# Dealing the first block of an output projection between the products of the delta rule's last tiles (1 core)

## The reference

```python
u = rms_norm(h, norm_mix)
proj = u @ w_in
pool_out = pool_mixer(proj[..., :512], ...)          # 1024 tokens x 512
gdn_out = gated_delta_net(q, k, v, z, a, b, ...)     # 1024 tokens x 512, 4 heads of 128
mix = concatenate([pool_out, gdn_out], axis=-1)      # 1024 x 1024
h = h + mix @ w_out                                  # the output projection
```

## Time and profile before

| what | value |
|---|---|
| median of 3 runs | 2611.97 us (2608.75 to 2614.02) |
| the profiled execution | 2618.43 us, its span 2616.7 us |
| PE busy | 2405.8 us, 92% of the span, 13848 products |
| DVE busy | 1825.9 us, 70% |
| ACT busy | 1076.6 us, 41% |
| GpSimd (POOL) busy | 720.0 us, 28% |
| mean granted clock of TensorE | 0.968 of 2.4 GHz |

### The profile page before, as it was taken

One profiled execution on the slowest core, in us unless ns is written; L12 is line 12 of the kernel. 1 busy time (PEld: TensorE's weight loads), 2 busy tenths in 40 slices (PEclk: granted clock), 3 DMA queues, 4 the chain that ended last, 5 costly groups with the idle time before them and its releaser, 6 DMA issues.

```text
span 2616.7 us, 35014 instructions
## 1 busy us (share of the span) xinstructions
PE 2405.8 (92%) x13848; PEld 1916.5 (73%) x13848; DVE 1825.9 (70%) x2431; ACT 1076.6 (41%) x1616; POOL 720.0 (28%) x737
## 2 busy tenths in 40 slices
PE   3988968869999999999999999898799999999998
PEld 3966823557778787888886668677687878888887
DVE  5358988884588798877865783465327688777775
ACT  5135378743343334443343441233224334444433
POOL 1432277505555111111032223334162320000000
PEclk8999979989999999999999999899799999999999
DMA  6200154224223634555422110000231344555442
GB/s 232 73 17 17 41 156 116 88 65 137 73 65 113 220 127 168 177 177 187 139 89 75 38 40 25 2 2 26 93 92 57 117 173 154 193 177 177 169 145 81
DMA packets 173849, 282.19 MB, mean 108 GB/s; under 512 B 13407, under 2 KB 86900, under 8 KB 173686
## 3 DMA queue, kind: packets, MB, share of 16 engines
q1 hardware_dynamic: 159184, 255.38, 30.4%
q10 hardware_dynamic: 14502, 24.58, 2.6%
HBM read 252.52 MB, written 27.33 MB: 107 GB/s over the span
## 4 chain that ended last, share of the span: by engine, by line
PE 38%; DVE 7%; issue 2%; ACT 2%; POOL 1%; ACTq 0%; DVEq 0%; POOLq 0%
PE ps L2884 10%; PE ps L2873 9%; PE ps L2572 2%; PE ps L2587 2%; PE ps L2574 2%; PE ps L2573 2%; PE ps L2589 2%; PE ps L2588 2%; PE ps L3052 2%; DVE yt L2400 2%; DVE yt L2389 1%; PE ps L3116 1%; PE ps L3107 1%; PE ps L3110 1%; PE ps L3026 0%
## 5 line engine op out<-in xcount | busy, mean ns | idle before, releaser
L1447 ACT ACTIVATE w_hi<-raw 128x1024 fp32r<-128x1024 f32 x198 | 209.0, 1057 | 365.7 <-DVE raw L2120 160.5
L2103 DVE TENSOR_TENSOR w_lo<-raw,w_hi 128x1024 fp32r<-128x1024 f32 x198 | 258.9, 1308 | 126.4 <-ACT w_hi L1447 126.1
L2884 PE MATMUL ps<-w_hi,us_hi 128*128 128x512 f32 x784 | 308.8, 394 | 17.4 <-DVE u_f L2129 10.0
L2884 PE MATMUL ps<-w_lo,us_hi 128*128 128x512 f32 x784 | 307.8, 393 | 0.0
L2884 PE MATMUL ps<-w_hi,us_lo 128*128 128x512 f32 x784 | 307.5, 392 | 0.0
L2572 PE MATMUL ps<-h_hi,w_hi 128*128 128x512 f32 x704 | 286.5, 407 | 8.8 <-issue 4.3
L2573 PE MATMUL ps<-h_lo,w_hi 128*128 128x512 f32 x704 | 276.6, 393 | 0.0
L2574 PE MATMUL ps<-h_hi,w_lo 128*128 128x512 f32 x704 | 276.4, 393 | 0.0
L2153 DVE TENSOR_TENSOR x<-x,ps 128x512 f32<-128x512 f32 x392 | 247.8, 680 | 0.0
L2587 PE MATMUL ps<-w_hi,h_hi 128*128 128x512 f32 (+2 forms) x512 | 184.2, 360 | 18.8 <-DVE h_lo L2513 7.3
L1012 POOL TENSOR_TENSOR raw<-raw,gate 128x1024 f32<-128x1024 f32 x32 | 93.5, 2945 | 377.3 <-DMA raw<-in_w_down_dram 377.3
(11 more groups left out here) (472 smaller groups left out, 5273.0 us busy)
## 6 DMA issues: line engine op xcount, KB each, us to landing
h_all<-h_t SPq DMA_DIRECT2D x96, 512.0 KB, 5.6
h_extra<-h_t SPq DMA_DIRECT2D x96, 512.0 KB, 6.8
raw<-in_w_up_dram SPq DMA_DIRECT2D x64, 512.0 KB, 3.9
raw<-in_w_down_dram SPq DMA_DIRECT2D x64, 512.0 KB, 5.9
raw<-in_w_ada_dram SPq DMA_DIRECT2D x48, 512.0 KB, 4.4
raw<-in_w_in_dram SPq DMA_DIRECT2D x32, 512.0 KB, 3.8
raw<-in_w_out_dram SPq DMA_DIRECT2D x32, 512.0 KB, 3.8
h_t<-ht_hi ACTq DMA_DIRECT2D x32, 256.0 KB, 2.3
```

The source lines that it names most:

```text
L1447: s.activation(w_hi[:, slot, :], raw[:, r, :], ACT.Copy).then_inc(sem("w_hi_done"), 1)
L2103: v.tensor_tensor(w_lo[:, slot, :], raw[:, r, :], w_hi[:, slot, :].bitcast(F32), ALU.subtract).then_inc(sem("split_done"), 1)
L2884: last = mm(ps[:, b, :], l[:, c, tok], r, start=(fresh and c == 0 and n == 0), stop=(c == 1 and n == 2), skip_group_check=True)
```

## The change

The first of the four blocks (tokens 0 to 511, columns 0 to 511) leaves `out_proj`. Its 32 parts (a weight piece kk, a token tile i and a row k, three products each) are dealt out in TensorE's loop over `GSTEPS`, behind the steps that `OUT_AFTER` names, tiles 0 and 1 into the banks of tile 5, tiles 2 and 3 into those of tile 6. The second block follows in banks 2, 3, 6 and 7 (`OUT_BANK`), behind tile 7's last step. For this:
- the eight pieces of `mix` for tokens 0 to 511 are copied by ACT behind eight `level_z` steps of tiles 5 to 7 (`MIX_HI_AT`) into `out_hi`, which lies over the values and the second half of the keys, and subtracted by DVE behind the `level_tu` steps of the same tiles and levels (`MIX_LO_AT`), in place;
- the first four weight splits go into GpSimd's loop, behind its product in (level_z, 7, 1) to (level_z, 7, 4), the first with the two waits that stood behind the loop;
- x comes back through SP: four loads ahead of the projection's fifth weight, after tile 7 has used its queries; four ahead of its 13th, after the first half's eight output tiles are complete (`wo_full`);
- the eight pieces for tokens 512 to 1023 stay where all 16 were.

```diff
@@ -226,2 +226,4 @@
         pm = at("pm", [P, GH, S], F32, AD)
+        out_hi = [at("out_hi_p", [P, GH, S], F32R, AU), at("out_hi_z", [P, GH, S], F32R, AX_ + 16 * K1)]
+        out_lo = [at("out_lo_p", [P, GH, S], F32R, AD), at("out_lo_z", [P, GH, S], F32R, AU + 16 * K1)]
         yt = at("yt", [P, 2, S], F32, AD + 16 * K1)
@@ -504,2 +506,12 @@
+        OUT_BANK = (4, 5, 0, 1, 2, 3, 6, 7)
+        OUT_PARTS = [(i, kk, k) for pair in ((0, 1), (2, 3)) for kk in range(4) for i in pair for k in range(2)]
+        OUT_AFTER = {("level_tu", 6, 5): 4, ("finish_c", 5, 0): 1, ("level_tu", 7, 3): 1, ("tail_b", 6, 0): 2,
+                     ("level_z", 7, 4): 1, ("chunk_b", 6, 0): 1, ("chunk_b", 6, 1): 1, ("level_z", 7, 5): 1, ("level_tu", 7, 5): 4,
+                     ("finish_c", 6, 0): 2, ("tail_b", 7, 0): 3, ("chunk_a", 7, 0): 2, ("chunk_b", 7, 0): 2,
+                     ("chunk_a", 7, 1): 2, ("chunk_b", 7, 1): 2, ("finish_b", 7, 0): 3}
+        assert sum(OUT_AFTER.values()) == len(OUT_PARTS)
+        MIX_HI_AT = {key: u for u, key in enumerate((("level_z", 6, 1), ("level_z", 5, 4), ("level_z", 6, 2), ("level_z", 5, 5),
+                                                     ("level_z", 6, 3), ("level_z", 7, 1), ("level_z", 6, 4), ("level_z", 7, 2)))}
+        MIX_LO_AT = {("level_tu", t, l): u for (_, t, l), u in MIX_HI_AT.items()}
         LAST_AT_W = max(t for t in range(NT) if t % SETS == 2)
@@ -841,2 +853,11 @@
                 last_of = [RAW[LAST][role] for role in LAST_ROLE]
+                if i == len(CH2) + 4:
+                    sp.wait_ge(prep_sem("mm", NT - 1), prep_count("mm", NT - 1, "kq"))
+                    sp.wait_ge(prep_sem("pool", NT - 1), prep_count("pool", NT - 1, "qdec"))
+                    for t in range(NT // 2):
+                        sp.dma_start(x[:, t, :], x_mid[t]).then_inc(sem("x_in0"), 16)
+                if i == len(CH2) + 12:
+                    sp.wait_ge(sem("wo_full"), 2 * NT + 8)
+                    for t in range(NT // 2, NT):
+                        sp.dma_start(x[:, t, :], x_mid[t]).then_inc(sem("x_in1"), 16)
                 sp.wait_ge(sem("split_done"), M_2 + i - 3 if i >= 4 else M_2 - 3 + last_of.index(i))
@@ -1150,6 +1171,9 @@
                     g.tensor_tensor(b[f"b{(l + 1) % 2}"], b["m"], hp(levelp[l + 1]), ALU.mult).then_inc(prep_sem("pool", t), 1)
+                    if t == NT - 1:
+                        if l == 1:
+                            pool.wait_ge(sem("scan_mm"), scan_count("mm", LAST_AT_W, "ai"))
+                            pool.wait_ge(sem("scan_dve"), scan_count("dve", LAST_AT_W, "sdec1"))
+                        split2(len(CH2) + l - 1)
-            pool.wait_ge(sem("scan_mm"), scan_count("mm", LAST_AT_W, "ai"))
-            pool.wait_ge(sem("scan_dve"), scan_count("dve", LAST_AT_W, "sdec1"))
-            for i in range(len(CH2), len(slots2)):
+            for i in range(len(CH2) + 4, len(slots2)):
                 split2(i)
@@ -1677,2 +1701,9 @@
                     s.activation(osum, osum, ACT.Sqrt, scale=1.0 / GD, bias=eps).then_inc(sem("scan_act"), 1)
+                if (kind, t, l) in MIX_HI_AT:
+                    u = MIX_HI_AT[kind, t, l]
+                    if u == 0:
+                        act.wait_ge(prep_sem("mm", 3), prep_count("mm", 3, "vtp"))
+                        act.wait_ge(sem("scan_dve"), scan_count("dve", 3, "gated"))
+                    s.activation(out_hi[u // GH][:, u % GH, 0:HALF], (pm, zc)[u // GH][:, u % GH, 0:HALF],
+                                 ACT.Copy).then_inc(sem("mix2_hi"), 1)
@@ -1680,5 +1711,3 @@
             act.wait_ge(sem("scan_dve"), scan_count("dve", NT - 1, "gated"))
-            for t in range(NT):
-                act.dma_start(x[:, t, :], x_mid[t]).then_inc(sem(f"x_in{t // 4}"), 16)
-            for u in range(2 * NK):
+            for u in range(NK, 2 * NK):
                 c, cols = u % NK, slice((u // NK) * HALF, (u // NK + 1) * HALF)
@@ -2078,4 +2107,4 @@
                     dve.wait_ge(sem(f"x_in{th}"), 192)
-                v.scalar_tensor_tensor(x[:, t, cols], x[:, t, cols], rs[:, t:t + 1], ps[:, n % 8, :], ALU.mult,
-                                       ALU.add).then_inc(sem("x_mixed"), 1)
+                v.scalar_tensor_tensor(x[:, t, cols], x[:, t, cols], rs[:, t:t + 1], ps[:, n % 8 if th else OUT_BANK[n], :],
+                                       ALU.mult, ALU.add).then_inc(sem("x_mixed"), 1)
@@ -2507,4 +2536,9 @@
                                            ALU.mult).then_inc(sem("scan_dve"), 1)
+                if (kind, t, l) in MIX_LO_AT:
+                    u = MIX_LO_AT[kind, t, l]
+                    dve.wait_ge(sem("mix2_hi"), u + 1)
+                    v.tensor_tensor(out_lo[u // GH][:, u % GH, 0:HALF], (pm, zc)[u // GH][:, u % GH, 0:HALF],
+                                    out_hi[u // GH][:, u % GH, 0:HALF].bitcast(F32), ALU.subtract).then_inc(sem("mix2_lo"), 1)
-            for u in range(2 * NK):
+            for u in range(NK, 2 * NK):
                 c, cols = u % NK, slice((u // NK) * HALF, (u // NK + 1) * HALF)
@@ -2579,3 +2613,3 @@
-            def tm(m, t, k0, width, hi, lo, start, stop, bank=None):
+            def tm(m, t, k0, width, hi, lo, start, stop, bank=None, ks=range(2)):
@@ -2584,3 +2618,3 @@
                 o = ps[:, t if bank is None else bank, 0:width]
-                for k in range(2):
+                for k in ks:
                     wh, wl = (w[:, r, 0:2 * width].rearrange("p (k n) -> p k n", k=2)[:, k, :] for w in (w_hi, w_lo))
@@ -2809,8 +2843,17 @@
                                 pe.wait_ge(sem("ln_sd"), 2)
-                            if blk == 1 and j == 0:
+                            if blk == 1 and th and j == 0:
                                 pe.wait_ge(sem("mix2_lo"), NK * th + 2 * (kk + 1))
                             for i in range(4):
+                                b = 4 * j + i
                                 if kk == 0 and th:
-                                    pe.wait_ge(sem(evicted), evicted_base + 4 * j + i + 1)
-                                last = tm(m - (M_2 if blk else 0), 4 * th + i, 2 * kk, HALF, h_hi, h_lo, kk == 0, kk == 3, 4 * j + i)
+                                    pe.wait_ge(sem(evicted), evicted_base + (OUT_BANK.index(b) if blk else b) + 1)
+                                if blk == 1 and th == 0:
+                                    if kk == 0 and i == 0:
+                                        pe.wait_ge(prep_sem("act", NT - 1), prep_count("act", NT - 1, "kct"))
+                                    if kk == 0 and i == 2:
+                                        pe.wait_ge(sem("scan_dve"), scan_count("dve", NT - 1, "gated"))
+                                    last = tm(m - M_2, i, 2 * (kk % 2), HALF, out_hi[kk // 2], out_lo[kk // 2], kk == 0, kk == 3,
+                                              OUT_BANK[b])
+                                else:
+                                    last = tm(m - (M_2 if blk else 0), 4 * th + i, 2 * kk, HALF, h_hi, h_lo, kk == 0, kk == 3, b)
                                 if kk == 3:
@@ -3031,2 +3074,3 @@
             pe.wait_ge(sem("z_silu"), GH - 1)
+            parts_done = 0
             for kind, t, l in GSTEPS:
@@ -3125,5 +3169,19 @@
                     turns(bank(7), ot).then_inc(sem("scan_mm"), 1)
+                for _ in range(OUT_AFTER.get((kind, t, l), 0)):
+                    i, kk, k = OUT_PARTS[parts_done]
+                    parts_done += 1
+                    if k == 0 and i == 0:
+                        pe.wait_ge(sem("split_done"), M_2 + len(CH2) + kk + 1)
+                        pe.wait_ge(sem("mix2_lo"), 2 * (kk + 1))
+                    if k == 0 and kk == 0 and i % 2 == 0:
+                        done = LAST_AT_W + i // 2
+                        pe.wait_ge(prep_sem("act", done), prep_count("act", done, "kct"))
+                    last = tm(len(CH2) + kk, i, 2 * (kk % 2), HALF, out_hi[kk // 2], out_lo[kk // 2], kk == 0 and k == 0, kk == 3 and k == 1,
+                              OUT_BANK[i], range(k, k + 1))
+                    if k == 1 and kk == 3:
+                        last.then_inc(sem("wo_full"), 1)
+                    elif k == 1 and i == 3:
+                        last.then_inc(sem("wo_part"), 1)
-            pe.wait_ge(sem("scan_dve"), scan_count("dve", NT - 1, "gated"))
-            out_proj(1, M_2 + len(CH2), (), "x_mixed", 2 * NT)
+            out_proj(1, M_2 + len(CH2), [(0, 0, kk) for kk in range(4)], "x_mixed", 2 * NT)
             mlp(1, M_MLP1, "x_mixed", 4 * NT, lambda part: None)
```

## The result

| | before | after |
|---|---|---|
| median | 2612.86 us (6 runs, 2608.75 to 2617.76) | 2588.90 us (6 runs, 2586.91 to 2596.54) |
| the profiled execution, its span | 2618.43, 2616.7 us | 2589.21, 2587.5 us |
| mean granted clock of TensorE | 0.968 | 0.971 |

The ratio is 0.991 with an interval of 0.9896 to 0.9925: 24.0 us faster by the medians, 19.6 to 27.2 by the interval. The forecast was 2588.0, with a range of 2580 to 2601.

The account below looks back on a forecast made before the run. The delta rule's end was taken as a latency chain with PE holes, the projection as PE-bound; 31.85 - 7.95 = 23.9 us gain took the 2611.97 us median to 2588, range 2580 to 2601.

Parts of the forecast that it names:

- the dealt products: 32 parts of 0.68 us among PE's steps of tiles 6 and 7: mostly in holes, +0.6, +1.1, -0.2, -1.2 by stretches.
- step 2: GpSimd's queue: first split ahead of the masked block for (level_z, 6, 5) makes PE wait, 4.05 us, bounds 0 and 4.6.
- What is removed: Stretch from tile 7's last turning (1864.51) to the projection's second block (1896.35) goes: 31.85 us.
- Copies and subtractions: Two ACT copies (1.1 us) and two DVE subtractions (1.2 us) lie on the chain: 2.3 us, bounds 0 and 2.3.
- S: How much later tile 7's last turning comes, added up along PE's order and taken off the gain: 7.95 us.
- The last 4 us: From tile 7's last product to its turning's end: GpSimd's split beside DVE delays the scaling, +1.3 us; undisturbed -0.15.
- Queues passed: SP's loads of x, late weights, GpSimd's later splits and DVE's evictions around the projection cost nothing.
- The rival of SP's queue: At half the load rate the first late projection weight comes late: 2 us lost, 2590 us; chance 0.04.
- stall and encounter: Rival: neither PE's wait for GpSimd's masked block nor DVE's slowed tile 7 scaling bites: 2583 us; chance 0.12.
- the rival on the clock: PE's lower clock holds to the delta rule's end: no gain, 2612 us (0.05); for half of it, 2600 us (0.12).
- some 6 us: Sign expected in the changed profile: the turning of tile 6 comes this much later against tile 5.
- signs of being wrong: PE waiting for splits between dealt parts or before the last weight, clock below 0.9 at the end, evictions awaiting x.

Follow-up runs that it names:

- The fourth run: Changed kernel with all 32 parts behind tile 7's last turning, copies, splits and x loads staying; 2609.21 us, ratio 0.9977 to the kernel before.
- the third run: Changed kernel with copies and subtractions of out_hi and out_lo moved to steps where ACT and DVE wait longer; 2593.76 us, ratio 0.9914 to the kernel before.
- the first run: Changed kernel with GpSimd making the masked block of (level_z, 6, 4) before it waits for the first split; 2586.42 us, ratio 0.9882 to the kernel before.
- the second run: Changed kernel with GpSimd holding the third split of the second block until tile 7's scaling is done; 2590.94 us, ratio 0.9901 to the kernel before.
- the fifth run: Changed kernel with masked block first, split held until tile 7's scaling, and copies and subtractions moved, all together; 2579.54 us, ratio 0.9875 to the kernel before.
- the sixth run: Changed kernel with the first four loads of x issued by ACT again instead of SP; 2589.36 us, ratio 0.9904 to the kernel before.

## Why the prediction was right

The time came out within 1 us of the forecast by the medians. That it is so close is luck: by the trace the gain was 21.4 where the sum said 23.9, and the interval of 19.6 to 27.2 us has room for both. The difference of 2.5 is almost all in two places, the dealt products (2.3) and the second block with its start (0.5); step 2 came out 0.3 smaller.

**What is removed** held: the projection's second block follows directly on the last turning, at full clock. The fourth run shows that the dealing carries it.

**1. Copies and subtractions**, 2.3 us: tile 5's first scan product comes 2.28 us later by the trace (26.03 us from tile 4's, before 23.75), and the third run takes 2.27 of it away. The chain that ended last in after goes through the two copies (0.52 each, at 1782.23 and 1783.02) and the two subtractions (0.69 and 0.70, at 1788.40 and 1794.64) that were named. The upper bound was the right choice.

**2. GpSimd's queue**, 4.05 us: 3.8 measured, with the wait at the very instruction named. S stood at 6.06 behind it (1811.48 + 7.73 against 1812.60 + 0.55; forecast 6.35), 3.8 more than the 2.28 of step 1.

**3. The dealt products**, forecast +0.3 in sum. This is the term that was mis-sized. The four parts ahead of tile 6's turning were "hidden", and cost 1.3 (S 7.37 at the turning, 1819.33): the wait of step 2 lets the clock fall, and the prediction had this only as a rival that takes half or all of the gain. It lasted some 5 us (1811.48 to 1816.53) and cost about 1.9 by the first run; with the parts' 2.72 that no longer fits into the hole of 3.1, about 1.5 are over by this count. Of the other stretches +0.7, +1.65, -0.4 and -0.6 were measured where +0.6, +1.1, -0.2 and -1.2 stood (the last sum holds a slip: its scan products add up to 7.3, not 7.2). S was 8.7 at tile 7's last product, not 6.65. PE's turnings and scan products that bound these stretches, and two parts between scan products:

```profile
1819.33 0.66 PE L3101 MATMUL ps<-ident,kc 128*128 128x128 f32 x4
...
1826.65 1.09 PE L3151 MATMUL ps<-state,kct 128*64 128x128 f32 x8
...
1842.83 0.60 PE L3101 MATMUL ps<-ident,kc 128*128 128x128 f32 x4
...
1849.49 1.09 PE L3151 MATMUL ps<-state,kct 128*64 128x128 f32 x8
...
1851.38 0.51 PE L2621 MATMUL ps<-w_hi,out_hi_p 128*128 128x512 f32 x1
...
1852.97 1.16 PE L3160 MATMUL ps<-vnew,kd 64*128 64x128 f32 x8
```

They show the second half of the error: a part was priced at 0.68 us, its share of a long run of equal products. Between scan products two parts took 1.59 (1851.38 to 1852.97) and not 1.36, and the six of the last stretch 4.76 and not 4.1. From 1826.65 to 1842.83 four parts that stand alone took 0.88 to 0.90 each up to the next product of another kind, and all eight there 6.42 instead of 5.44. PE shows no wait in these stretches, so what is over adds to S. Why the change between the kinds of product costs this was not tried.

**4. The last 4 us**, +1.3: the scaling was to end 4.8 us after the last product and the turning 5.4; they ended 4.88 (1863.61 + 2.63 - 1861.36) and 5.35 after. S = 9.93. The encounter that the earlier trace rows had shown for other instructions came here too, and the second run shows the scaling at 0.69 with the split held. By the Trainium skill, page "SBUF — State Buffer", section "Who interferes with whom", such a pair excludes one another for a whole instruction. The trace agrees with it here (2.63 us, up to 0.55 behind the end of GpSimd's subtraction). The rule would have given the same sum.

**5. Queues passed**, nothing: the issue of SP in after shows the second half of x ahead of the last four weights:

```profile
1889.06 1.76 SPq L862 DMA_DIRECT2D x<-x_mid  x4
1890.87 2.72 SPq L864 DMA_DIRECT2D raw<-in_w_out_dram  x4
```

The first late weight's cast starts at 1898.80, 9.9 us behind the end of the first half's products (10 were worked out), and PE shows no wait between 1885 and 1963. The rival of SP's queue falls. So do the others: stall and encounter both bit; the lower clock ended before the dealt products had passed tile 6's turning, far from the point at which it would have cost the gain, and no dealt part waited for its weight or its subtraction (the only such wait, 0.88 us, is in the first and the fifth run, where the split comes later).

The reading of the earlier trace rows behind the rival on the clock was not exact: tile 7's first scan product still takes 1.09 us at 1847.91, so the 2.02 at 1858.39 does not follow the long wait ahead of the turning. Waits of 0.7 to 0.8 us lie between the two, and the dealt products fill those as well.

Two things were not in the sum. The second block takes 0.4 us longer, 22.36 us from its first product to the eighth eviction (1866.71 to 1889.07) where before it took 21.96: its first half runs at 0.233 us a product instead of 0.227, and its first product lasts 0.08 us longer. And before it began at 1896.26, 0.1 us ahead of the 1896.35 of the forecast.

**Sum by the trace:** 31.85 - 0.1 - 9.93 - 0.4 = 21.4.

**The signs.** The wait, the slow scaling, the full clock and the second block without a cold start came as named. Tile 6's turning came 5.1 us later against tile 5's first scan product (22.46 us behind it, before 17.37). The "some 6 us" there did not follow from the forecast's own sum, in which 2.3 of the 6.35 lie ahead of tile 5. The eighth eviction came at 1896.8 with the 7.73 added, and 1894 stood. None of the signs of being wrong was seen.

## What to carry to other kernels

Work without waits that is dealt into the holes of a chain of latencies gains twice: its own time, and the clock that the holes had cost; 19.5 of the block's 21.8 us were won so. What it costs stands in the queues it is threaded through: look, for every instruction that a wait now precedes, at what is queued behind it and who needs that first, since here one masked block of 0.7 us, issued behind a split instead of ahead of it, cost nearly 5. Price a small piece of work where it will stand: three products cost 0.68 us in a long run and up to 0.90 alone between others. Two engines that slow each other, as DVE and GpSimd did here, can be kept apart by one wait on the one that has time to spare, and the repairs added up here (8.8 us singly, 8.9 together), each having its own place on the path.

## What the runs showed of the hardware

- After the same wait of 3.65 us the granted clock came back at different moments: the first dealt product took 0.50 us in the second and the sixth run, 0.79 in the changed kernel and the third run. From tile 5's first scan product to tile 6's the four took 29.08, 29.04, 29.78 and 30.08 us.
- At full clock long runs of the projection's products have two paces, and the pace goes with the operand, a few products late. In after three products that read `out_hi_p` and `out_lo_p` took 0.70 us at 1867.02 (0.233 each), three that read `out_hi_z` and `out_lo_z` 0.68 at 1880.03 (0.227). What runs on the other engines does not decide it. In after, the second and the fifth run the pace changes at the same place in the block; DVE falls idle near that moment in after, and in the other two it goes on for another 3.5 us beside GpSimd's splits. In the fourth run, where both operands come twice ahead of the second block, the pace goes to and fro with them, first without any split on GpSimd and then, from 1884.30 on, beside its splits. Why the operand matters was not tried.

```profile
1867.02 0.40 PE L2622 MATMUL ps<-w_lo,out_hi_p 128*128 128x512 f32 x1
...
1867.72 0.40 PE L2622 MATMUL ps<-w_lo,out_hi_p 128*128 128x512 f32 x1
...
1880.03 0.39 PE L2621 MATMUL ps<-w_hi,out_hi_z 128*128 128x512 f32 x1
...
1880.71 0.39 PE L2621 MATMUL ps<-w_hi,out_hi_z 128*128 128x512 f32 x1
```
